# One product of 512 columns in place of two of 256 for the attention's weights times values, with a second addition on VectorE

## The chip, the cores and the metric

The kernel runs on one core of a Trainium2 chip. The metric is the device time of one execution in microseconds (us), the median of several runs. All work is in 4-byte floats. The engines are named as in the profile: PE is TensorE's matmul, PEld its load of the stationary operand, DVE is VectorE, ACT ScalarE, POOL GpSimd, SP SyncE.

## The reference, cut to what matters

One layer of a decoder is computed for a prompt of 1024 tokens and for 8 samples of 8 tokens. The change touches only the attention over the prompt: 8 heads of 64, in blocks of 128 queries, with stick-breaking weights in place of a softmax.

```
z = q @ k.T * HEAD_DIM ** -0.5 + bias
log_beta = log_sigmoid(z)
log_stay = where(causal, log_beta - z, 0)
log_after = reverse_cumsum(log_stay) - log_stay
w = where(causal, exp(log_beta + log_after), 0)
o = w @ v
```

The last line, `w @ v`, is what is done in another way. Before and after it there are dense projections (the input projection ahead of it and beside it, gates, output and feed-forward layers behind it), which the change leaves alone.

## The kernel before, in words

A product of two 4-byte operands is made out of reduced-precision products: each operand is split into a high part (a rounded copy, type fp32r) and a low part (the rest), and high by high, high by low and low by high are added in PSUM. The dense projections (L1126, 364 columns at a time) are such triples.

The heads are taken two at a time: four head pairs, i = 0 to 3, and for each of them 18 dense chunks of the input projection. A unit is one head and one block of 128 queries, so a head pair has 16 units; they come in pairs of the same head and neighbouring query blocks, with 8, 8, 6, 6, 4, 4, 2 and 2 blocks of keys. The order of all engines' work is a list written out ahead (`order`), from which each engine takes its own part, and semaphores hold them together. Slot n of the list has, for different units at once:

- `logits` of unit n+1 on PE (L1276), into banks that the `cap` of the unit before must have read;
- `cap` on DVE (L1893, L1894), `softplus` on ACT (two activations), `suffix` on DVE (the scan L1901 and the subtraction L1903), `weights` on ACT (L1610);
- `turn`: PE transposes the weights in groups of up to four blocks (L1286), ACT copies the result as the high part `th` (L1625), and DVE makes the low part `tl` (`low`, L1911);
- `av`: PE multiplies. The stationary operand `v` is a block of 128 keys by 128 columns, the high part of the 64 values in one half and the low part in the other. The moving operand is `th` and then `tl`, 256 columns (two query blocks), and all blocks of keys are added in 256 columns of bank 7 (`AVB`). For the last block of keys (`top`) only one of the two query blocks exists, so there it is 128 columns;
- `out`: the two halves of the partitions must be added. ACT copies the low half to `otmp` (L1634), and DVE adds it to the high half and writes the result into `br` (L1930). There is one `out` for each pair of units, 8 in a head pair, 32 in all.

Between these, PE has dense products as a filler in every slot. An engine works strictly down its list: what stands behind a waiting instruction waits too. `av` waits for `tl_made` (DVE) and, in a unit pair's first group, for `o_made` of the unit pair before; `logits` waits for `zc_ready` (DVE); `turn` waits for `w_made` (ACT).

Of the kernel before, what the change touches and what calls it, by code (L numbers as in the profile page):

```python
# [33 lines left out]
F32R = mybir.dt.float32r  # L34
I32 = mybir.dt.int32
ALU = mybir.AluOpType
ACT = mybir.ActivationFunctionType

P = 128
# [4 lines left out]
GRAN = 4  # L44
# [6 lines left out]
def ds(start, size):  # L51
    return bass.ds(start, size)


def hybrid_layer(nc, x_prompt, x_sample, cache_k, cache_v, state_conv, page_table, norm1_w, w_in, conv_w,
# [42 lines left out]
    with ctx:  # L98
# [3 lines left out]
        def place(name, shape, dt, at=None):  # L102

            size = 4
            for n in shape[1:]:
                size *= n
            off = cursor[0] if at is None else at
            if at is None:
                cursor[0] += (size + 31) // 32 * 32
            return nc.alloc_sbuf_tensor_at(name, shape, dt, offset=off)  # L110
# [85 lines left out]
        vcu = place("vcu", [P, NV], F32)  # L196
        vhl = place("vhl", [P, NB * 2 * P], F32R)
        sp = [place(f"sp{s}", [P, SEQ], F32) for s in range(2)]
        th = [place(f"th{s}", [P, GRAN * 2 * P], F32R) for s in range(NT)]
        tl = [place(f"tl{s}", [P, GRAN * 2 * P], F32R) for s in range(NT)]  # L200
        stage = [place(f"stage{s}", [P, GRAN * P], F32) for s in range(2)]
        otmp = place("otmp", [P, 2 * P], F32)
        ends = place("ends", [P, NPAIR * N_END], F32)
# [26 lines left out]
        def blocks(t, n=P):  # L230
            return t.rearrange("p (k n) -> p k n", n=n)
# [13 lines left out]
        def bank(b, a=0, e=512):  # L245
            return ps[:, b * 512 + a:b * 512 + e]
# [8 lines left out]
        def sem(name, credit=0):  # L255

            s = ctx.enter_context(nc.semaphore(name))
            if credit:
                credits.append((s, credit))
            return s  # L260
# [24 lines left out]
        stage_made = sem("stage_made")  # L285
        stage_out = [sem(f"stage_out{s}", 1) for s in range(2)]
        vh_made, v_made = sem("vh_made"), sem("v_made")
        otmp_made, o_made = sem("otmp_made"), sem("o_made")
        qs_made, ks_made, k_copied = sem("qs_made"), sem("ks_made"), sem("k_copied")
        cols_in, cols_turned, cols_made = sem("cols_in"), sem("cols_turned"), sem("cols_made")  # L290
        pad_made, conv_step = sem("pad_made"), sem("conv_step")
# [825 lines left out]
        def _(pe):  # L1117
# [77 lines left out]
            for e in order:  # L1195
# [92 lines left out]
                elif e[0] == "av":  # L1288
# [9 lines left out]
                    for b in range(a, z):  # L1298
                        v = vhl[:, (b * 2 + h) * P:(b * 2 + h + 1) * P]
                        x = P if b == top else 0  # L1300
                        at = (b - a) * 2 * P
                        mm(bank(AVB, x, 2 * P), v, th[s][:, at + x:at + 2 * P], start=(b == 0), stop=False)  # L1302
                        ins = mm(bank(AVB, x, 2 * P), v, tl[s][:, at + x:at + 2 * P], start=False, stop=(b == top))  # L1303
                    ins.then_inc(turned_used, 1)


# [456 lines left out]
        def _(v):  # L1763
# [98 lines left out]
            for e in order:  # L1862
# [33 lines left out]
                elif e[0] == "suffix":  # L1896
                    u = e[2]
                    W = width(u)
                    rev = sp[u % 2][:, 0:W][:, ::-1]
                    v.wait_ge(sp_made, i * UNITS + u + 1)  # L1900
                    V_.tensor_tensor_scan(rev, rev, rev, 0.0, ALU.add, ALU.bypass).then_inc(suffix_made, 1)  # L1901
                    v.wait_ge(suffix_made, i * UNITS + u + 1)
                    V_.tensor_tensor(zc[u % NZ][:, 0:W], zc[u % NZ][:, 0:W], sp[u % 2][:, 0:W], ALU.subtract).then_inc(arg_made, 1)  # L1903
                elif e[0] == "low":
                    u, j = e[2:]
                    turn = ("turn", i, u, j)
                    a, z = groups(u)[j]
                    s = both_turned((i, u), j) % NT
                    x = UNIT[u][1] % 2 * P
                    v.wait_ge(th_made, w_no[turn] + 1)  # L1910
                    V_.tensor_tensor(blocks(tl[s], 2 * P)[:, 0:z - a, x:x + P], blocks(bank(TURN + turn_no[turn] % 2, 0, (z - a) * P)),  # L1911
                                     f32(blocks(th[s], 2 * P)[:, 0:z - a, x:x + P]), ALU.subtract).then_inc(tl_made, 1)
                elif e[0] == "v_split":
                    m = 3 + e[2]
                    s = m % 2
                    v.wait_ge(stage_made, i * 6 + m + 1)
                    if e[2] < 2:
                        src = stage[s][:, :].rearrange("p (b h d) -> p b h d", h=2, d=HD)
                        dst = vhl[:, e[2] * GRAN * 2 * P:(e[2] + 1) * GRAN * 2 * P].rearrange("p (b x d) -> p b x d", x=4, d=HD)
                        V_.tensor_copy(dst[:, :, 0:4:3, :], src).then_inc(vh_made, 1)  # L1920
                        v.wait_ge(vh_made, i * 2 + e[2] + 1)
                        V_.tensor_tensor(dst[:, :, 1:3, :], src, f32(dst[:, :, 0:4:3, :]), ALU.subtract).then_inc(v_made, 1)
                    else:
                        V_.tensor_copy(vs[:, ds(i * P, P)], stage[s][0:SMP, 0:P]).then_inc(v_made, 1)
                elif e[0] == "out":
                    u = e[2]
                    h, t = UNIT[u]
                    r = slice(h * HD, h * HD + HD)
                    v.wait_ge(otmp_made, i * NB + u // 2 + 1)
                    V_.tensor_tensor(br[r, ds(i * NTOK + (4 * NTOK + t // 2 * (2 * P)), 2 * P)], ps[r, AVB * 512:AVB * 512 + 2 * P],  # L1930
                                     otmp[r, :], ALU.add).then_inc(o_made, 1)
                elif e[0] == "p1_end":
                    p1_over(v)
                    v.wait_ge(bias_in, 16 * (P // NEW))
                    v.wait_ge(const_step, N_STEPS)
                    V_.memset(qblk[:, :], 0.0).then_inc(qblk_zero, 1)
                    v.wait_ge(qblk_zero, 1)
                    v.wait_ge(qs_made, NPAIR)
                    own_q(0)
                elif e[0] == "page":  # L1940
                    _, j, t = e
                    if by_dve(t):
                        kct_free(v, j, t)
                        v.wait_ge(s_turned, s_no[e] + 1)
                        V_.tensor_copy(blocks(kct[t // GRAN % 2][:, :], 512)[:, :, t % GRAN * P:(t % GRAN + 1) * P],
                                       blocks(bank(TURN + s_no[e] % 2))).then_inc(kct_dve, 1)
                elif e[0] == "s_cap":
                    j = e[1]
                    new = "s_new", j
                    v.wait_ge(s_turned, s_no[new] + 1)  # L1950
                    V_.scalar_tensor_tensor(out=zs_c[:, PAST:KEYS], in0=bank(TURN + s_no[new] % 2, 0, SMP), scalar=bias_s[:, 0:1],
                                            in1=new_cap[:, ds(j * SMP, SMP)], op0=ALU.add, op1=ALU.min).then_inc(new_z_read, 1)
                    V_.tensor_scalar(zs_c[:, 0:PAST], ps[:, ZB * 512:ZB * 512 + PAST], bias_s[:, 0:1], Z_MAX,
                                     ALU.add, ALU.min).then_inc(s_zc, 1)
                    if j + 1 < NITER:
                        own_q(j + 1)
                elif e[0] == "b_split":
                    x = b_part(e[1])
                    v.wait_ge(b_hi, e[1] + 1)
                    V_.tensor_tensor(bl[:, x], br[:, b_source(e[1])], f32(bh[:, x]), ALU.subtract).then_inc(b_lo, 1)  # L1960
                elif e[0] == "b_split_sample":
                    v.wait_ge(b_hi, KT + 1)
                    V_.tensor_tensor(b_sample(bl), b_sample(br), f32(b_sample(bh)), ALU.subtract).then_inc(b_lo, 1)
                elif e[0] == "s_suffix":
                    j = e[1]
                    rev = sp_s[:, :][:, ::-1]
                    v.wait_ge(s_sp, j + 1)
                    V_.tensor_tensor_scan(rev, rev, rev, 0.0, ALU.add, ALU.bypass).then_inc(s_suffix, 1)
                    v.wait_ge(s_suffix, j + 1)
                    V_.tensor_tensor(zs_c[:, :], zs_c[:, :], sp_s[:, :], ALU.subtract).then_inc(s_arg, 1)  # L1970
                elif e[0] == "s_out":
                    _, j, n = e
                    v.wait_ge(s_turned, s_no[e] + 1)
                    for h in range(2):
                        r = slice(h * HD, h * HD + HD)
                        own = n * 2 * NEW + h * NEW
                        src = bank(TURN + s_no[e] % 2, 0, P)[r, :].rearrange("p (w x) -> p w x", x=TILE)[:, :, own:own + NEW]
                        dst = blocks(br[r, :], NTOK)[:, NPAIR:2 * NPAIR, ds(j * (2 * NEW) + (SEQ + n * NEW), NEW)]
                        ins = V_.tensor_copy(dst, src)
                    ins.then_inc(so_made, 1)  # L1980
# [157 lines left out]
```

## Time and profile before

| | |
|---|---|
| median of 3 runs | 1657.03 us (1656.65 to 1657.3) |
| profiled execution, its own time | 1656.68 us |
| its span | 1654.7 us |
| PE busy | 1644.6 us (99%) |
| DVE busy | 694.0 us (42%) |
| ACT busy | 516.9 us (31%) |
| granted TensorE clock | 0.999 of full speed |
| `av` products | 79.6 to 444.3 us of the span |

The duration of one matmul in the profile is its way through the array and is longer than its share of time: matmuls overlap, and what one costs is read from start to start. Idle time of an engine stands in square brackets behind the instruction that ended it, with the one that it waited for.

### The profile page before, as it was taken

The numbers are of one execution on the slowest core, as the hardware profiler recorded it, in microseconds if no ns is written. First come the engines' busy times: TensorE is split into PE (matmuls) and PEld (weight loads), VectorE is DVE, ScalarE is ACT, GpSimd is POOL, SyncE is SP. The second block draws the span as 40 slices with busy tenths as digits, with TensorE's granted clock in tenths as the row PEclk, the third lists the DMA queues.
The fourth block names the chain that finished last, engine by engine and source line by source line (L and its number), as shares of the span: only waits on it lengthen the run. The fifth ranks groups of instructions, "written<-read, shape, count | busy, mean of one in ns | idle before, by whom it ended". The sixth has DMA issues, their size and how long they took to land.

```text
span 1654.7 us, 24985 instructions
## 1 busy us (share of the span) xinstructions
PE 1644.6 (99%) x9956; PEld 1520.6 (92%) x9956; DVE 694.0 (42%) x1156; ACT 516.9 (31%) x1001; POOL 569.2 (34%) x402
## 2 busy tenths in 40 slices
PE   9999999999999999999999999999999999999998
PEld 8999999999988889999889998899888998899987
DVE  7785868859421222466334330032211331022333
ACT  7565655656322222422245220022100220012111
POOL 5212212112212111232884334733347324652510
PEclk9999999999999999999999999999999999999999
DMA  5202112021276677442552111321113111221211
GB/s 161 66 26 68 39 39 73 21 63 42 96 241 196 208 230 228 164 143 91 172 178 77 52 52 64 102 65 50 53 64 115 49 42 64 89 83 46 89 51 57
DMA packets 145006, 157.55 MB, mean 95 GB/s; under 512 B 9119, under 2 KB 99899, under 8 KB 144892
## 3 DMA queue, kind: packets, MB, share of 16 engines
q1 hardware_dynamic: 144746, 155.93, 29.7%
q8 instruction: 79, 1.29, 0.3%
q14 instruction: 35, 0.29, 0.1%
q10 hardware_dynamic: 146, 0.04, 0.0%
HBM read 136.96 MB, written 18.98 MB: 94 GB/s over the span
## 4 chain that ended last, share of the span: by engine, by line
PE 89%; DVE 6%; ACT 3%; issue 1%; POOL 0%; DVEq 0%; ACTq 0%; POOLq 0%
PE ps L1126 51%; PE ps L1418 10%; PE ps L1423 10%; PE ps L1421 9%; DVE sp L1901 2%; PE ps L1320 2%; DVE zc L1893 1%; PE ps L1276 1%; PE ps L1286 1%; PE ps L1364 1%; PE ps L1332 1%; ACT sp L1604 1%; PE ps L1303 1%; PE ps L1302 1%; DVE br L1849 1%
## 5 line engine op out<-in xcount | busy, mean ns | idle before, releaser
L1126 PE MATMUL ps<-xh,wh 128*128 128x364 f32 (+1 forms) x956 | 323.7, 339 | 0.7 <-DVE xl L1874 0.6
L1126 PE MATMUL ps<-xh,wl 128*128 128x364 f32 (+1 forms) x956 | 313.8, 328 | 0.0
L1126 PE MATMUL ps<-xl,wh 128*128 128x364 f32 (+1 forms) x956 | 313.8, 328 | 0.0
L1113 POOL TENSOR_TENSOR wl<-raw,wh 128x1024 fp32r<-128x1024 f32 x106 | 256.3, 2418 | 19.1 <-POOL wh L1110 18.9
L1126 PE MATMUL ps<-yh,wh 128*128 128x384 f32 (+1 forms) x768 | 250.5, 326 | 0.2 <-DVE yl L2070 0.2
L1126 PE MATMUL ps<-yh,wl 128*128 128x384 f32 (+1 forms) x768 | 250.5, 326 | 0.0
L1110 POOL CAST wh<-raw 128x1024 fp32r<-128x1024 f32 x106 | 111.1, 1048 | 404.8 <-issue 383.1
L1126 PE MATMUL ps<-yl,wh 128*128 128x384 f32 (+1 forms) x768 | 250.3, 326 | 0.0
L1728 ACT ACTIVATE ts<-tt 128x384 f32<-128x384 f32 (+1 forms) x96 | 48.8, 508 | 553.8 <-DVE tt L2082 553.7
L1027 POOL CAST wh<-raw 128x1024 fp32r<-128x1024 f32 x48 | 50.8, 1059 | 479.1 <-issue 205.3
L1126 PEld LDWEIGHTS ps<-xh,wh 128*128 128x128 f32 x956 | 179.7, 188 | 17.0 <-issue 15.3
L2018 DVE TENSOR_TENSOR x<-ps,x 128x512 f32<-128x512 f32 x90 | 60.0, 690 | 320.5 <-PE ps L1423 302.2
L1126 PEld LDWEIGHTS ps<-xl,wh 128*128 128x128 f32 x956 | 180.1, 188 | 0.7
L1126 PEld LDWEIGHTS ps<-xh,wl 128*128 128x128 f32 x956 | 179.7, 188 | 0.0
L1418 PE MATMUL ps<-wh,hh 128*128 128x512 f32 x468 | 179.0, 390 | 0.6 <-POOL wl L1113 0.6
L1423 PE MATMUL ps<-wl,hh 128*128 128x512 f32 x468 | 163.4, 389 | 0.0
L1421 PE MATMUL ps<-wh,hl 128*128 128x512 f32 x416 | 161.9, 389 | 0.0
L1036 POOL TENSOR_TENSOR wl<-raw,wh 128x1024 fp32r<-128x1024 f32 x48 | 116.6, 2428 | 97.2 <-DVE zc L1903 91.4
L2082 DVE TENSOR_SCALAR tt<-ps 128x384 f32<-128x384 f32 (+1 forms) x96 | 51.4, 535 | 233.0 <-PE ps L1126 231.6
L1126 PEld LDWEIGHTS ps<-yh,wh 128*128 128x128 f32 x768 | 144.1, 188 | 1.0 <-issue 0.4
L1126 PEld LDWEIGHTS ps<-yl,wh 128*128 128x128 f32 x768 | 144.1, 188 | 0.0
L1126 PEld LDWEIGHTS ps<-yh,wl 128*128 128x128 f32 x768 | 144.1, 188 | 0.0
(190 smaller groups left out, 2632.2 us busy)
## 6 DMA issues: line engine op xcount, KB each, us to landing
raw<-in_w_down SPq DMA_DIRECT2D x112, 256.0 KB, 2.9
raw<-in_w_in SPq DMA_DIRECT2D x80, 256.0 KB, 3.5
cache<-in_cache_k SPq DMA_DIRECT2D x64, 256.0 KB, 3.6
cache<-in_cache_v SPq DMA_DIRECT2D x64, 256.0 KB, 3.7
raw<-in_w_up SPq DMA_DIRECT2D x64, 256.0 KB, 3.2
raw<-in_w_out SPq DMA_DIRECT2D x48, 256.0 KB, 2.9
gates<-gst SPq DMA_DIRECT2D x16, 544.0 KB, 6.0
gb<-gates SPq DMA_DIRECT2D x16, 544.0 KB, 5.7
```

The lines of the kernel that those rows point to most:

```text
L1027: g.tensor_copy(wh[s][:, :], raw[s][:, :]).then_inc(w_hi, 1)
L1036: g.tensor_tensor(wl[s][:, :], raw[s][:, :], f32(wh[s][:, :]), ALU.subtract).then_inc(w_split, 1)
L1110: g.tensor_copy(high[:, :], raw[n % 3][:, :]).then_inc(w_hi, 1)
L1113: g.tensor_tensor(low[:, :], raw[n % 3][:, :], f32(high[:, :]), ALU.subtract).then_inc(w_split, 1)
L1126: ins = mm(out, lhs[:, k * P:(k + 1) * P], rhs[:, x], start=(first and a == 0 and m == 0), stop=(last and a == n - 1 and m == 2))
L1320: ins = tr(bank(tb, p * P, (p + 1) * P), cache[g][:, (a * NPAIR + p) * P:(a * NPAIR + p + 1) * P], ident[:, :])
L1418: mm(out, hi, w, start=k == 0, stop=False)
L1421: mm(out, low[:, k * SEQ + b * P:k * SEQ + b * P + P], w, start=False, stop=False)
L1423: return mm(out, hi, lo_w, start=False, stop=last)
L1728: A(ts_[m % 2][:, 0:z - a], tt[:, 0:z - a], ACT.Square).then_inc(s_made, 1)
L2018: V_.tensor_tensor(x, step_bank(step_no[g, b, h]), x, ALU.add).then_inc(step_free, 1)
L2082: V_.tensor_scalar(tt[:, 0:z - a], step_bank(t, 0, z - a), 0.0, None, ALU.max).then_inc(step_free, 1)
```

## The change

The high and the low part of the turned weights now lie in one tile, `thl`, the low part behind the high one. Each block of keys is one matmul with the high and the low columns side by side as its moving operand: 512 columns, and 256 (written 2x128) for the last block. Bank 7 then holds the products with the high part in its first 256 columns and those with the low part in its last 256. The stationary operand is loaded once instead of twice. `out` has one more addition on DVE: first the high half of the last 256 columns is added to `otmp` (in place), and, after a wait on a new semaphore for that, `otmp` to the high half of the first 256 columns as before. The product of the values' low part with the weights' low part is computed too, as before, but is no longer added to the result.

```diff
-        th = [place(f"th{s}", [P, GRAN * 2 * P], F32R) for s in range(NT)]
-        tl = [place(f"tl{s}", [P, GRAN * 2 * P], F32R) for s in range(NT)]
+
+        thl = [place(f"thl{s}", [P, 2 * GRAN * 2 * P], F32R) for s in range(NT)]
+        th = [w[:, 0:GRAN * 2 * P] for w in thl]
+        tl = [w[:, GRAN * 2 * P:2 * GRAN * 2 * P] for w in thl]
...
-                        mm(bank(AVB, x, 2 * P), v, th[s][:, at + x:at + 2 * P], start=(b == 0), stop=False)
-                        ins = mm(bank(AVB, x, 2 * P), v, tl[s][:, at + x:at + 2 * P], start=False, stop=(b == top))
+                        ins = mm(blocks(bank(AVB, 0, 4 * P), 2 * P)[:, :, x:2 * P], v,
+                                 blocks(thl[s], GRAN * 2 * P)[:, :, at + x:at + 2 * P], start=(b == 0), stop=(b == top))
...
                     v.wait_ge(otmp_made, i * NB + u // 2 + 1)
+                    V_.tensor_tensor(otmp[r, :], ps[r, AVB * 512 + 2 * P:AVB * 512 + 4 * P], otmp[r, :], ALU.add).then_inc(otmp_both, 1)
+                    v.wait_ge(otmp_both, i * NB + u // 2 + 1)
                     V_.tensor_tensor(br[r, ds(i * NTOK + (4 * NTOK + t // 2 * (2 * P)), 2 * P)], ps[r, AVB * 512:AVB * 512 + 2 * P],
                                      otmp[r, :], ALU.add).then_inc(o_made, 1)
```

PE at the first `av` of the program (head pair 0, units 0 and 1, the first group of four blocks and the start of the second), before:

```order
L1126 MATMUL ps<-xl,wh_61 128x364
L1126 MATMUL ps<-xh,wl_63 128x364
L1302 MATMUL ps<-th_124,vhl 128x256
L1303 MATMUL ps<-tl_126,vhl 128x256
L1302 MATMUL ps<-th_124,vhl 128x256
L1303 MATMUL ps<-tl_126,vhl 128x256
```

And in the changed kernel, where two lines more stand ahead of the same code:

```order
L1128 MATMUL ps<-xl,wh_61 128x364
L1128 MATMUL ps<-xh,wl_63 128x364
L1304 MATMUL ps<-thl_124,vhl 128x512 x4
L1304 MATMUL ps<-thl_125,vhl 128x512 x3
L1304 MATMUL ps<-thl_125,vhl 128x2x128
L1288 MATMUL ps<-ident,zc_132 128x128 x8
```

The 16 matmuls of this `av` have become 8, in the same place between the same neighbours.

DVE at the third `out` of head pair 0, between two small copies of the convolution and a low part, before:

```order
L1849 SCALAR_TENSOR_TENSOR br<-vcu,cols,br 128x1024
L1849 SCALAR_TENSOR_TENSOR br<-vcu,cols,br 128x64
L1930 TENSOR_TENSOR br<-ps,otmp 64x256
L1911 TENSOR_TENSOR tl_126<-ps,th_124 128x4x128
L1911 TENSOR_TENSOR tl_127<-ps,th_125 128x128
L1901 SCALAR_TENSOR_TENSOR sp_123<-sp_123 128x384
```

And in the changed kernel:

```order
L1851 SCALAR_TENSOR_TENSOR br<-vcu,cols,br 128x1024
L1851 SCALAR_TENSOR_TENSOR br<-vcu,cols,br 128x64
L1932 TENSOR_TENSOR otmp<-ps,otmp 64x256
L1934 TENSOR_TENSOR br<-ps,otmp 64x256
L1913 TENSOR_TENSOR thl_124<-ps,thl_124 128x4x128
L1913 TENSOR_TENSOR thl_125<-ps,thl_125 128x128
L1903 SCALAR_TENSOR_TENSOR sp_123<-sp_123 128x384
```

Nothing has changed places; one addition stands ahead of the old one, and everything behind it on DVE has one instruction more before it.

## Rows read from the trace of the kernel before

**Rows 1.** The page: span, and busy time of each engine.
```profile
span 1654.7 us, 24985 instructions
...
PE 1644.6 (99%) x9956; PEld 1520.6 (92%) x9956; DVE 694.0 (42%) x1156; ACT 516.9 (31%) x1001; POOL 569.2 (34%) x402
```

**Rows 2.** One line's instructions, L1303: count, shortest, median, longest ns, first and last start, forms.
```profile
L1303 PE MATMUL ps<-tl,vhl x160: 274/283/289, 79.7 to 444.3; 128*128 128x256 f32 x128, 128*128 128x128 f32 x32
```

**Rows 3.** Timeline of PE, one av of eight blocks: start, duration (us), instruction.
```profile
79.60 0.28 PE L1302 MATMUL ps<-th,vhl 128*128 128x256 f32 x1
79.72 0.28 PE L1303 MATMUL ps<-tl,vhl 128*128 128x256 f32 x1
...
81.27 0.22 PE L1302 MATMUL ps<-th,vhl 128*128 128x128 f32 x1
...
81.45 1.06 PE L1286 MATMUL ps<-ident,zc 128*128 128x128 f32 x8
```

**Rows 4.** PE's busy time, instructions and clock in a stretch of 512-column matmuls only.
```profile
1590.00:1640.00 50.00, 50.00 (x222) 1.00 0.19 69
```

**Rows 5.** Busy time by stretch: length, PE, PEld, DVE, ACT, POOL, clock, DMA share, GB/s.
```profile
98.40:126.00 27.60, 27.45 (x187) 26.52 (x186) 26.11 (x51) 16.56 (x36) 3.87 (x4) 1.00 0.07 20
126.00:150.00 24.00, 24.00 (x153) 23.87 (x152) 10.87 (x25) 12.86 (x34) 9.23 (x5) 1.00 0.15 45
```

**Rows 6.** Timeline of DVE in head pair 0, second to sixth out; last, head pair 3.
```profile
98.40 0.43 DVE L1930 TENSOR_TENSOR br<-ps,otmp 64x256 f32<-64x256 f32 x1 [1.00 <-ACT otmp L1634]
...
101.63 0.88 DVE L1911 TENSOR_TENSOR tl<-ps,th 128x512 fp32r<-128x512 f32 x2
...
110.59 0.41 DVE L1930 TENSOR_TENSOR br<-ps,otmp 64x256 f32<-64x256 f32 x1
110.92 0.87 DVE L1911 TENSOR_TENSOR tl<-ps,th 128x512 fp32r<-128x512 f32 x2
...
113.56 0.34 DVE L1894 SCALAR_TENSOR_TENSOR zc<-ps,bias_p,diag_cap 128x128 f32<-128x128 f32 x1
...
115.92 0.43 DVE L1930 TENSOR_TENSOR br<-ps,otmp 64x256 f32<-64x256 f32 x1 [0.21 <-ACT otmp L1634]
...
118.36 0.56 DVE L1911 TENSOR_TENSOR tl<-ps,th 128x384 fp32r<-128x384 f32 x1
...
123.89 0.40 DVE L1930 TENSOR_TENSOR br<-ps,otmp 64x256 f32<-64x256 f32 x1
124.34 0.56 DVE L1911 TENSOR_TENSOR tl<-ps,th 128x384 fp32r<-128x384 f32 x1
...
131.54 0.43 DVE L1930 TENSOR_TENSOR br<-ps,otmp 64x256 f32<-64x256 f32 x1 [0.89 <-ACT otmp L1634]
132.00 0.29 DVE L1911 TENSOR_TENSOR tl<-ps,th 128x128 fp32r<-128x128 f32 x1
...
433.47 0.29 DVE L1911 TENSOR_TENSOR tl<-ps,th 128x128 fp32r<-128x128 f32 x1
```

**Rows 7.** Timeline of PE and its loads at the matmuls behind those; last, head pair 3.
```profile
102.16 0.33 PE L1126 MATMUL ps<-xh,wl 128*128 128x364 f32 x1
...
102.46 0.35 PE L1302 MATMUL ps<-th,vhl 128*128 128x256 f32 x1
...
113.96 0.38 PE L1276 MATMUL ps<-kx,qd 128*128 128x256 f32 x1
...
119.06 0.35 PE L1302 MATMUL ps<-th,vhl 128*128 128x256 f32 x1
...
125.09 0.19 PEld L1302 LDWEIGHTS ps<-th,vhl 128*128 128x128 f32 x1
...
132.41 0.19 PEld L1302 LDWEIGHTS ps<-th,vhl 128*128 128x128 f32 x1
...
435.25 0.29 PE L1302 MATMUL ps<-th,vhl 128*128 128x256 f32 x1
```

More of the change, by code:

```diff
@@ L287, in hybrid_layer @@
         vh_made, v_made = sem("vh_made"), sem("v_made")
-        otmp_made, o_made = sem("otmp_made"), sem("o_made")
+        otmp_made, otmp_both, o_made = sem("otmp_made"), sem("otmp_both"), sem("o_made")
         qs_made, ks_made, k_copied = sem("qs_made"), sem("ks_made"), sem("k_copied")
```

## The prediction

> **What bounds the kernel now.** I read the page first. PE is busy for 1644.6 us of a span of 1654.7 [rows 1], so the kernel is bound by PE nearly everywhere, and a change is worth what it takes from or adds to PE's stream: matmul time, or time in which PE waits. The matmuls that change, 160 blocks of keys, lie in the first quarter of the span, from 79.6 to 444.3 us [rows 2], and there I looked for the engine that PE would wait for. The busy time by stretches names it. From the second `out` of head pair 0 to 126 us DVE is busy for 26.11 us of 27.60, against 10.87 of 24.00 in the stretch behind [rows 5]. In the first of these two DVE has no slack to speak of, while PE still looks full (27.45). The timelines of both engines then show how close they run: the next sections go through them.
>
> **What it takes from PE.** An `av` of eight blocks has 14 matmuls of 256 columns in 81.27 - 79.60 = 1.67 us, 0.119 us each, and its two matmuls of 128 columns take 81.45 - 81.27 = 0.18 us [rows 3]. Matmuls of 512 columns, where there is nothing else, come every 50.00 / 221 = 0.226 us [rows 4]. So a full block goes from 2 x 0.119 to 0.226 us and saves 0.012 us; the number of columns is the same, and only the fixed part of one matmul goes away. The second load of the stationary operand costs nothing before either: it runs beside the matmul. The last block goes from 0.18 us to one matmul of 256 columns, 0.12 us, and saves 0.06 us. With 128 full and 32 last blocks [rows 2] that is 1.5 + 1.9 = 3.4 us for PE in all, 0.14, 0.12, 0.10 and 0.07 us for an `av` of eight, six, four and two blocks.
>
> No row shows a moving operand of two pieces 1024 elements apart. I take it at the price of a contiguous one, 0.226, since the columns are the same in number and bank 7 is written in one piece. The bound on the other side is two matmuls of 256 columns, 0.238: then the full blocks save nothing and 1.9 us are left.
>
> The trace is to be weighed against a rule here. The Trainium skill, page "TensorE: Matmul & The Clock Gate", section "Back-to-back issue gap", gives a sustained 81 ns per matmul of 128 columns and 131 ns for 512, so that wide matmuls would be far cheaper per column; by an estimate between its two figures a block would go from about 195 to 131 ns, and PE would save some 8 us on the full blocks. The rows give 226 ns, so the trace does not agree, and the sum goes by the rows.
>
> **What it adds to DVE.** 32 additions of 64x256 from PSUM, the same shape as the one that is there, which takes 0.40 to 0.43 us [rows 6]. The new one is followed by a wait for its own end, so it counts in full with the semaphore's way: 0.45 us, the step from the `out` at 123.89 to the low part at 124.34, or from 131.54 to 132.00 (0.46) [rows 6]. The lower bound is the step where the next instruction does not have to wait, 110.59 to 110.92, 0.33 us [rows 6]. I take 0.45, since the second addition reads what the first writes. In all 14.4 us on DVE; the question is how much of it reaches PE. The Trainium skill, page "VectorE: DVE Perf Modes", section "The DRAIN you can't avoid", says that a semaphore between two instructions costs nothing beyond the pipeline's own drain; by it the two additions without a wait ahead of the old successor would cost 0.33 each, 0.12 less. The rows show both steps, 0.33 and 0.45, and the forecast uses the longer.
>
> **Which of the eight places reach PE.** The eight `out`s of a head pair, in order:
>
> - The first is absorbed: before the second DVE has stood idle for 1.00 us [rows 6].
> - The second (98.40) has the scan, the subtraction and the low part at 101.63 behind it, and PE already waits for that low part: from 102.16 to 102.46 it takes 0.30 us where the pace of 364 columns is 0.167 [rows 6, 7]. So all of 0.45 reaches PE.
> - The third (110.59) stands before the `cap` that ends at 113.56 + 0.34 = 113.90, and PE starts the logits that need it at 113.96 [rows 6, 7]: 0.45 again.
> - The fourth (115.92) stands before the low part that ends at 118.36 + 0.56 = 118.92; PE's `av` starts at 119.06 [rows 6, 7]: 0.45. The 0.21 us of idle before it is a wait for ACT, which itself runs behind DVE there, and gives nothing back.
> - The fifth (123.89) stands before the low part that ends at 124.90; PE's load for the `av` comes at 125.09, 0.19 us later [rows 6, 7]; the next case shows 0.12 to be enough. Slack 0.07, so 0.38 reaches PE.
> - The sixth (131.54) stands directly before the low part that ends at 132.29, and PE loads at 132.41 [rows 6, 7]: 0.45. In head pair 3 PE comes to this `av` only at 435.25, with the low part made at 433.47 + 0.29 = 433.76, so there it is absorbed [rows 6, 7].
> - The seventh and eighth are absorbed: DVE is less than half busy there [rows 5].
>
> Between the second and the fifth DVE never catches up, as its busy share shows, and what PE saves in the `av`s there only makes it wait longer. So per head pair PE loses 3 x 0.45 + 0.38 + 0.45 = 2.18 us (1.73 in head pair 3). It keeps its saving where it is the bound: two `av`s of eight, one of four, two of two blocks, 2 x 0.14 + 0.10 + 2 x 0.07 = 0.52 us. Net 3 x 1.66 + 1.21 = 6.2 us more.
>
> The other stages are not touched, and all of them come behind PE, so the delay stays. The profiled execution took 1656.68 us and the median is 1657.03, 0.35 above; on the median the sum is 1657.0 + 6.2 = 1663.2, and I say 1663.
>
> What is queued behind the new wait on DVE is what was named for each place; PE's `av` also waits for `o_made`, which comes 0.45 us later, but it is made before the low part for which the same `av` waits, so it is not what is late. ACT's next copy to `otmp` waits for `o_made` too, a slot later.
>
> **The rivals.**
>
> - *DVE's additions stay hidden.* For it: DVE is busy for only 42% of the span [rows 1], and at two of the places DVE stands idle for 1.00 and 0.89 us right before [rows 6]. Against it: 102.46 and 113.96, where PE waits for DVE already. It decides if PE's stops there are made by something else that has slack. Time: 1657.0 - 3.4 = 1653.6. A wide matmul that is cheaper than 0.226 would take it lower: at 0.20 by 128 x 0.026 = 3.3 us more, 1650.3. Chance 0.08 for both together, since the rows speak against both. The rule of the Trainium skill on the sustained pace, above, is of this second kind.
> - *Half of it is absorbed.* The added instruction costs 0.33 in place of 0.45, and one or two of the places have a slack that I don't see: 4 x (3 x 0.33 - 0.52) = 1.9, 1658.9, within what can't be told from no change. Chance 0.20.
> - *All additions reach PE*: 32 x 0.45 = 14.4 less the saving of 3.4 is +11, 1668. A PE that is held up more often would set this off, since `logits`, `turn` and `av` hand on a delay in a ring (PE, DVE, ACT, PE). Chance 0.07.
> - The forecast, five places (four in the last head pair), 1660.4 to 1666: chance 0.65.
>
> **The numbers.** A measurement of this kernel tells about 0.2%, 3.3 us, from no change. Slower by more than that is the forecast and the rival above it, 0.72; within it 0.20; faster 0.08, since even the full saving of 3.4 us is only just past the bound. The range: down to 1658, which takes in most of the half-absorbed case, up to 1667, the forecast's upper end and part of the last rival. The price of the addition (0.33 to 0.46) alone moves the sum by 19 x 0.12 = 2.3 us.
>
> **What the profile after would show.** `av` of eight blocks in about 1.72 us where it was 1.85; 512 columns from start to start in 0.226 to 0.23 us. The new addition 0.40 to 0.43 us, the old one 0.45 behind it. PE's stop before the `av` behind the second `out` 0.6 us long where it was 0.13, and one of about 0.5 us more before the logits behind the third; each head pair some 1.6 us longer. No second stop at the seventh and eighth. I would be wrong if PE's stops do not grow by the addition's length at 102.46 and 113.96 (then something else holds it), or if the wide matmul's pace is not that of 512 contiguous columns.

## The result, and the profile after

The changed kernel takes 1672.37 us (median of 4, 1670.36 to 1672.76), the kernel before 1657.16: a ratio of 1.0089, 95% interval 1.0072 to 1.0107. It is slower by 15.2 us. The forecast was 1663 with a range of 1658 to 1667: the direction was right, the size was not. The profiled execution took 1670.36 us, the shortest of the four; its span is 13.7 us longer than that of [rows 1].

What the prediction had worked out is there. The page's two lines that answer to [rows 1]:

```profile
span 1668.4 us, 24697 instructions
...
PE 1646.4 (99%) x9796; PEld 1512.5 (91%) x9796; DVE 717.0 (43%) x1188; ACT 516.4 (31%) x1001; POOL 568.6 (34%) x402
```

PE has 160 matmuls fewer. The timeline of PE at the `av` of eight blocks, which answers to [rows 3], and at the first place where it waited for DVE, which answers to the first two rows of [rows 7]:

```profile
79.42 1.87 PE L1304 MATMUL ps<-thl,vhl 128*128 128x512 f32 x8
81.13 1.03 PE L1288 MATMUL ps<-ident,zc 128*128 128x128 f32 x8
...
101.75 0.33 PE L1128 MATMUL ps<-xh,wl 128*128 128x364 f32 x1
102.50 0.70 PE L1304 MATMUL ps<-thl,vhl 128*128 128x512 f32 x2 [0.42 <-DVE thl L1913]
```

The `av` takes 81.13 - 79.42 = 1.71 us (forecast 1.72), which is seven matmuls of 512 columns at 0.227 us and one of 256 at 0.12, and the matmul before the next one stands for 0.75 us where its pace is 0.167, a stop of 0.58 (forecast 0.6, 0.13 before).

What the prediction had not worked out stands 30 us later. The timeline of DVE and POOL from the sixth `out` of head pair 0 on answers to the last rows of [rows 6]:

```profile
132.62 0.43 DVE L1932 TENSOR_TENSOR otmp<-ps,otmp 64x256 f32<-64x256 f32 x1 [0.89 <-ACT otmp L1636]
133.08 0.43 DVE L1934 TENSOR_TENSOR br<-ps,otmp 64x256 f32<-64x256 f32 x1
133.54 0.29 DVE L1913 TENSOR_TENSOR thl<-ps,thl 128x128 fp32r<-128x128 f32 x1
133.65 1.04 POOL L1029 CAST wh<-raw 128x1024 fp32r<-128x1024 f32 x1 [4.19 <-issue]
133.75 1.21 DVE L1903 TENSOR_TENSOR_SCAN sp<-sp 128x128 f32<-128x128 f32 x1
134.86 2.40 POOL L1038 TENSOR_TENSOR wl<-raw,wh 128x1024 fp32r<-128x1024 f32 x1 [0.18 <-POOL wh L1029]
134.99 2.42 DVE L1905 TENSOR_TENSOR zc<-zc,sp 128x128 f32<-128x128 f32 x1
```

The same places in the kernel before:

```profile
132.21 0.41 DVE L1901 TENSOR_TENSOR_SCAN sp<-sp 128x128 f32<-128x128 f32 x1
132.66 0.29 DVE L1903 TENSOR_TENSOR zc<-zc,sp 128x128 f32<-128x128 f32 x1
132.81 1.04 POOL L1027 CAST wh<-raw 128x1024 fp32r<-128x1024 f32 x1 [4.45 <-issue]
134.03 2.40 POOL L1036 TENSOR_TENSOR wl<-raw,wh 128x1024 fp32r<-128x1024 f32 x1 [0.18 <-POOL wh L1027]
```

A scan of 128 columns takes 1.21 us in place of 0.41, and a subtraction of 128 columns 2.42 in place of 0.29. Both end just behind an instruction of POOL: the scan at 134.96, behind the cast's end at 134.69, the subtraction at 137.41, behind 137.26. Before, DVE was through at 132.95, as POOL's cast had just begun. Of the scan's own 0.41 us 0.27 lie behind POOL's end, of the subtraction's own 0.29 us 0.15 do: in both, all but 0.14 us of the instruction's own duration comes only when POOL is done. POOL's own instructions keep their 1.04 and 2.40 us. At half speed each, DVE's subtraction would have been through after some 0.6 us. The Trainium skill, page "SBUF — State Buffer", section "Who interferes with whom", says that a DVE instruction with two inputs in SBUF contends with a GpSimd instruction that reads SBUF, for a read interface that the two share, and its section "SBUF: two separate sides" that it is a lock and not a split of bandwidth; the trace agrees in both, by the figures just given. An instruction that reads one of its inputs from PSUM is not held: in the kernel before, POOL's subtraction runs from 134.03 to 136.43, and DVE's `qz` inside it takes 1.08 us, as it does at 139.65 in the changed kernel, where POOL is idle:

```profile
135.20 1.08 DVE L1798 SCALAR_TENSOR_TENSOR qz<-ps,qd 64x364 fp32r<-64x364 f32 x2 [2.25 <-ACT qd L1535]
```

The kernel before has a hold of this kind too, 11 us earlier. Its scan of 256 columns, which takes 0.68 us elsewhere, takes 0.96 here and ends 0.54 behind a cast of POOL (120.89 + 1.04 = 121.93):

```profile
120.89 1.04 POOL L1027 CAST wh<-raw 128x1024 fp32r<-128x1024 f32 x1 [16.60 <-DVE zc L1903]
...
121.51 0.96 DVE L1901 TENSOR_TENSOR_SCAN sp<-sp 128x256 f32<-128x256 f32 x1
```

The chain of waits of the changed kernel shows what this delay does (start, length, what):

```profile
134.99 2.43 DVE zc L1905
...
137.66 0.07 ACT qd L1537
...
140.20 0.55 DVE qz L1800
140.75 0.14 issue
140.88 1.23 PE ps L1128 x6
```

ACT works strictly down its list: the exponential of unit 15 (L1612) waits for the subtraction, and behind it stand the copies of the next head pair's queries (`qd`, L1537), which begin at 137.66 where they began at 133.20. DVE's `qz` waits for them, and PE for the bank that `qz` frees:

```profile
138.63 0.27 PE L1288 MATMUL ps<-ident,zc 128*128 128x128 f32 x1
140.88 0.40 PE L1128 MATMUL ps<-xh,wh 128*128 128x364 f32 x1 [1.98 <-DVE qz L1800]
```

The waits of PE in the stretch 79:450 are, in the changed kernel (who waited for whom: us in all, times, longest):

```profile
PE ps L1128 <- DVE qz L1800: 5.9, 3, 2.0
PE ps L1304 <- DVE thl L1913: 5.4, 15, 0.5
PE ps L1278 <- DVE zc L1896: 1.1, 4, 0.3
```

The last two lines are the kind of wait that the forecast had, though not quite in its places. At the third `out` it had one stop of about 0.5 us before the logits. The trace has two, 0.22 us before the low part's `av` at 112.22 and 0.26 before the logits at 114.43, and the second is there without any addition as well (0.25 at 114.00 in the first experiment): PE comes earlier by what the product saves. The first line is new and occurs once in each of head pairs 0 to 2, since behind the last one there are no next queries to copy. In head pair 0 the matmul before the stop starts at 138.63 and the one behind it at 140.88, 2.25 us later; less the 0.06 us of a 128-column matmul, a stop is 2.2 us.

There is a third part. The granted clock, 1.00 in the whole of the stretch before, fell for 3.4 us after the second of these stops. Windows of the changed kernel (length, PE busy and instructions, clock, DMA share, GB/s):

```profile
240.00:245.00 5.00, 3.59 (x22) 1.00 0.34 96
245.00:250.00 5.00, 4.43 (x17) 0.66 0.04 12
...
245.90:249.20 3.30, 3.30 (x13) 0.50 0.00 0
```

At 0.50, which is 1.2 GHz of 2.4, PE did 13 matmuls in 3.30 us; without the stop it does 22 in the same window (shown below). The first 13 matmuls behind this stop take 3.78 us (245.57 to 249.35), those behind the third stop, at full clock, 2.23 (351.81 to 354.04): the stretch costs some 1.5 us. The granted clock over the span is 0.998 in this profiled execution (1670.36 us) and 0.997 in the other three (1672.28 to 1672.76), which fits one more such stretch in each of them: 3.3 us at half clock lower the mean by 0.001. They have no trace that shows it, and they are longer by 1.9 to 2.4 us, which is more than one stretch.

### The profile page after: what moved, and what is told of

It reads as the page before. It is cut to its first block, busy times and chain, and to the rows that moved or that the text cites. A ratio compares the mean times of both kernels' runs of the same rounds, so it can differ in the third digit from the quotient of the medians.

```text
span 1668.4 us, 24697 instructions
## 1 busy us (share of the span) xinstructions
PE 1646.4 (99%) x9796; PEld 1512.5 (91%) x9796; DVE 717.0 (43%) x1188; ACT 516.4 (31%) x1001; POOL 568.6 (34%) x402
## 4 chain that ended last, share of the span: by engine, by line
PE 82%; DVE 11%; ACT 4%; issue 2%; POOL 0%; DVEq 0%; ACTq 0%; POOLq 0%
PE ps L1128 46%; PE ps L1420 10%; PE ps L1425 10%; PE ps L1423 9%; DVE sp L1903 3%; PE ps L1322 2%; DVE thl L1913 1%; DVE zc L1895 1%; DVE zc L1905 1%; PE ps L1304 1%; PE ps L1366 1%; PE ps L1334 1%; ACT sp L1606 1%; PE ps L1278 1%; DVE br L1851 1%
```

## The experiments

The first four kernels take the two halves of the change apart, take the collision away, and put one addition at one place. Each time is given with that of the kernel before as it was measured beside it.

**The wide product alone.** The second addition is left out, so the product with the weights' low part is made but not added.

```diff
                     v.wait_ge(otmp_made, i * NB + u // 2 + 1)
-                    V_.tensor_tensor(otmp[r, :], ps[r, AVB * 512 + 2 * P:AVB * 512 + 4 * P], otmp[r, :], ALU.add).then_inc(otmp_both, 1)
-                    v.wait_ge(otmp_both, i * NB + u // 2 + 1)
```

> The changed kernel without the second addition in `out` (the product with the weights' low part is made but not added to the result). Forecast's terms: only PE's saving is left, 3.4 us in all, of which the 0.12 us and 0.10 us of the av products in the stretch where DVE sets the pace only make PE wait longer, so 2 us at least: 1653.6 to 1655. If a moving operand of two pieces 1024 elements apart is dearer than a contiguous one (rival): av of eight blocks takes 1.85 us or more and the time is 1657 or above.

Measured: 1654.79 us (1654.29 to 1655.06) against 1656.57, ratio 0.9988 (0.9979 to 0.9997). The product gives back 1.8 us. That is the forecast's term for the places where PE is the bound, 4 x 0.52 = 2.1; a dearer operand of two pieces is out. From the first `av` to the first dense matmul behind the last one the profile has 362.80 us, against 364.81 before. The `av` of eight blocks takes 81.59 - 79.86 = 1.73 us:

```profile
79.86 1.90 PE L1304 MATMUL ps<-thl,vhl 128*128 128x512 f32 x8
81.59 0.27 PE L1288 MATMUL ps<-ident,zc 128*128 128x128 f32 x1
```

POOL and DVE already touch here, without an addition: the cast begins at 132.49, 0.32 us earlier than before, and the subtraction at 132.53 takes 1.14 us. PE has no stop for `qz` from it.

**The addition alone**, on the kernel before: the old addition is made twice, the second waiting for the first.

```diff
+                    if u in (1, 3, 5, 7, 9, 11, 13, 15):
+                        V_.tensor_tensor(br[r, ds(i * NTOK + (4 * NTOK + t // 2 * (2 * P)), 2 * P)], ps[r, AVB * 512:AVB * 512 + 2 * P],
+                                         otmp[r, :], ALU.add).then_inc(otmp_both, 1)
+                        v.wait_ge(otmp_both, i * 8 + (1, 3, 5, 7, 9, 11, 13, 15).index(u) + 1)
```

> The kernel before with one more 64x256 addition of the same shape on DVE in every `out`, the old one waiting for it; the products stay as before. Theory of the collision (DVE's scan and subtraction behind the sixth `out` now fall on POOL's split of the V weights, stand still until it is over, and ACT and then PE wait): the whole loss is here, 1672 to 1676, with PE standing some 2 us near 138.6, 243 and 350 us. Rival, the product is what costs: 1657 to 1664.

Measured: 1664.95 us (1664.69 to 1668.61), ratio 1.0049 (1.0034 to 1.0065). My expectation of 1672 to 1676 was wrong, and the profile says why: here the starts of DVE's scan and of POOL's cast lie within hundredths of a microsecond, and one execution has it go either way. The profiled execution is the slow one of the four, 1668.61; the timelines of DVE and POOL in its head pairs 0 and 2:

```profile
134.06 1.04 POOL L1027 CAST wh<-raw 128x1024 fp32r<-128x1024 f32 x1 [4.29 <-issue]
134.08 1.30 DVE L1901 TENSOR_TENSOR_SCAN sp<-sp 128x128 f32<-128x128 f32 x1
135.42 2.40 DVE L1903 TENSOR_TENSOR zc<-zc,sp 128x128 f32<-128x128 f32 x1
...
344.64 1.26 POOL L1027 CAST wh<-raw 128x1024 fp32r<-128x1024 f32 x1 [4.30 <-issue]
344.65 0.41 DVE L1901 TENSOR_TENSOR_SCAN sp<-sp 128x128 f32<-128x128 f32 x1
345.10 0.95 DVE L1903 TENSOR_TENSOR zc<-zc,sp 128x128 f32<-128x128 f32 x1
```

In head pair 0, and likewise in head pair 1, POOL got its way, and the whole collision follows; PE has two stops of 2.0 us. In head pair 2 DVE did, as the durations show, although the cast's start is written 0.01 us ahead of the scan's: the scan runs at its usual 0.41, the cast is the longer one (1.26 in place of 1.04), and the subtraction is held only to the cast's end, 0.95. The other three executions (1664.69 to 1664.97) are 8.1 to 8.4 us above the kernel before, which is the forecast's price of the additions without any collision: 6.2 net and 2.1 of saving make 8.3. They have no trace; that they had no stop for `qz` is inferred from this sum and from the 3.7 us between them and the profiled one, nearly two stops.

**The collision taken away.** The changed kernel, with POOL's split of the V weights held back until DVE has done the subtraction of unit 15.

```diff
             def high_before(n):
 
                 i, k = divmod(n, 6)
+                if k == V and i > 0:
+                    return i - 1, 15
                 return (i - 1, 11) if k == K else None
```

> The changed kernel with one more condition on POOL: the high part of the V weights (head pairs 1 to 3) is made only when DVE has finished the subtraction of unit 15 of the head pair before. Theory of the collision: the scan and subtraction behind the sixth `out` take 0.41 and 0.29 us again, PE's three stops of 2.2 us are gone and so are the stretches at half clock that they bring: 1661 to 1664, near the forecast's 1663. Rival, the additions are handed on in a ring of PE, DVE and ACT and POOL has nothing to do with it: the stops stay, 1672.

Measured: 1663.32 us (1663.08 to 1663.51), ratio 1.0040 (1.0024 to 1.0055), 9.05 us below the changed kernel and 6.75 above the kernel before, where the forecast's sum was 6.2. (The changed kernel was 15.2 us above the kernel before as measured beside it; by that the wait takes away 8.5 us.) The timeline of DVE and POOL, and PE's window that had been at half clock:

```profile
134.85 0.41 DVE L1905 TENSOR_TENSOR_SCAN sp<-sp 128x128 f32<-128x128 f32 x1
135.30 0.29 DVE L1907 TENSOR_TENSOR zc<-zc,sp 128x128 f32<-128x128 f32 x1
...
135.85 1.04 POOL L1029 CAST wh<-raw 128x1024 fp32r<-128x1024 f32 x1 [5.31 <-DVE zc L1907]
```

```profile
245.90:249.20 3.30, 3.30 (x22) 1.00 0.00 0
```

and PE's waits, with no line for `qz`:

```profile
PE ps L1306 <- DVE thl L1915: 5.5, 15, 0.5
PE ps L1280 <- DVE zc L1898: 1.1, 4, 0.3
```

The profiles close the sum. From the first `av` to the first dense matmul behind the last one there are 364.81 us before, 370.67 here and 378.75 in the changed kernel. Without the collision that is 5.9 us more, by the forecast 6.2. The collision adds 8.1, and three stops of 2.2 us and one stretch at half clock make 3 x 2.2 + 1.5 = 8.1. From the scan of unit 15 in head pair 0 to that in head pair 1 there are 100.91 us before, 102.49 here (1.6 more, as forecast) and 104.69 in the changed kernel, 2.20 more again.

The ring of PE, DVE and ACT as a cause of its own is out: the additions are all still there, and 9 of the 15 us are gone with one wait on POOL.

**One addition, in the sixth `out` only**, on the kernel before (the same edit as above with `if u in (11,)`).

> The kernel before with the extra addition only in the sixth `out` of each head pair. The scan behind it then starts at about 132.66, 0.15 us ahead of POOL's cast at 132.81, and the subtraction at 133.1, in the cast. Theory of the collision: the subtraction is held to the cast's end at 133.85 but is through before POOL's own subtraction at 134.03, so the stop of PE is short, 0 to 0.4 us: 3 x (0.45 + 0 to 0.4) = 1.4 to 2.6, 1658.4 to 1659.6. Forecast without any collision: 1658.4. If the collision is already whole here: 3 x 2.6 = 8 and some loss of clock, 1665 to 1669.

Measured: 1658.10 us (1657.73 to 1658.60) against 1656.57, ratio 1.0009 (0.9999 to 1.0018): 1.5 us, as the forecast's 3 x 0.45 has it, at the edge of what the measurement tells. The scan is ahead of the cast and takes 0.41, the subtraction behind it 0.94:

```profile
132.89 0.41 DVE L1901 TENSOR_TENSOR_SCAN sp<-sp 128x128 f32<-128x128 f32 x1
133.03 1.11 POOL L1027 CAST wh<-raw 128x1024 fp32r<-128x1024 f32 x1 [4.45 <-issue]
133.34 0.94 DVE L1903 TENSOR_TENSOR zc<-zc,sp 128x128 f32<-128x128 f32 x1
```

**Two additions in the sixth `out`**, the same edit with the addition in a loop of two.

> The kernel before with two extra additions in the sixth `out` of each head pair, one more than in the run before. Theory of the collision: the scan behind them now starts near 133.3, after POOL's cast at about 133.0, so it is held to the cast's end and the subtraction to the end of POOL's own subtraction; PE stops for some 2 us in head pairs 0 to 2, and each such stop can bring 3.4 us at half clock, which cost 1.6: 3 x (0.9 + 2.0) = 8.7 and up to 3 x 1.6, so 1665 to 1670. Without a collision the price stays that of waiting in line: 3 x 0.9 = 2.7, 1659.3.

Measured: 1665.77 us (1665.27 to 1665.91) against 1656.80, ratio 1.0053 (1.0038 to 1.0068): 9.0 us. The second addition costs 7.5 us where the first cost 1.5. The timeline of DVE and POOL:

```profile
133.26 1.04 POOL L1027 CAST wh<-raw 128x1024 fp32r<-128x1024 f32 x1 [4.44 <-issue]
133.59 0.99 DVE L1901 TENSOR_TENSOR_SCAN sp<-sp 128x128 f32<-128x128 f32 x1
134.61 2.40 DVE L1903 TENSOR_TENSOR zc<-zc,sp 128x128 f32<-128x128 f32 x1
```

and of PE's waits the one for `qz`:

```profile
PE ps L1126 <- DVE qz L1798: 5.0, 3, 1.7
```

The step lies where the scan's start passes the cast's. The granted clock did not fall in this profiled execution, although PE stood idle for 1.7 us three times; so the stops bring the fall in some cases only.

**The additions at the second to fifth `out`** (`if u in (3, 5, 7, 9)`).

> The kernel before with the extra addition only in the second to fifth `out` of each head pair, where DVE sets the pace. Forecast's terms: 4 x (3 x 0.45 + 0.38) = 6.9, 1663.5, PE's stops behind the second, third and fourth `out` longer by the addition; DVE meets PE again at 128 us and there is no collision. Rival (the additions cost only in the sum of all): less than 1660.

Measured: 1663.17 us (1662.76 to 1663.50), ratio 1.0038 (1.0025 to 1.0052): 6.4 us of the forecast's 6.9. The four places are measured only together.

**At the first, seventh and eighth** (`if u in (1, 13, 15)`).

> The kernel before with the extra addition only in the first, seventh and eighth `out` of each head pair. Forecast's terms: absorbed, 1656.6 to 1657.2, no stop of PE that was not there before. If DVE's idle time there is not slack: up to 12 x 0.45 = 5.4, 1662.

Measured: 1656.97 us (1656.67 to 1657.64), ratio 1.0001 (0.9992 to 1.0010): absorbed. The three parts, 1.5, 6.4 and 0.2, make 8.1 us, what the additions cost together without a collision.

**The wide product only where its addition is absorbed.** The second addition stands behind the same `if u in WIDE`.

```diff
+        WIDE = (1, 13, 15)
...
+                        if u in WIDE:
+                            ins = mm(blocks(bank(AVB, 0, 4 * P), 2 * P)[:, :, x:2 * P], v,
+                                     blocks(thl[s], GRAN * 2 * P)[:, :, at + x:at + 2 * P], start=(b == 0), stop=(b == top))
+                        else:
+                            mm(bank(AVB, x, 2 * P), v, th[s][:, at + x:at + 2 * P], start=(b == 0), stop=False)
+                            ins = mm(bank(AVB, x, 2 * P), v, tl[s][:, at + x:at + 2 * P], start=False, stop=(b == top))
```

> The wide product and the second addition only for the first, seventh and eighth pair of units of each head pair (av of eight, two and two blocks), where the additions should be absorbed; the other pairs of units as before. Forecast's terms: 4 x (0.14 + 0.07 + 0.07) = 1.1 us less than before, 1655.5, with everything that is absorbed staying so. If the additions are not absorbed there: 1657 or above.

Measured: 1655.86 us (1655.35 to 1657.21) against 1656.80, ratio 0.9995 (0.9986 to 1.0004). It is 0.9 us less by the medians, which the measurement can't tell from nothing.

**Control: POOL's extra wait on the kernel before.**

> Control for the run in which POOL's split of the V weights waits for DVE's subtraction of unit 15: the same condition on the kernel before. Theory of the collision: before, the scan and subtraction are through at 132.95 and the cast starts at 132.81, so there is hardly a collision to remove: 1656.5 to 1657.3. If the condition is worth something by itself (rival: the gain of 9 us in that run came from POOL's later work, not from the collision): 1655 or below.

Measured: 1656.94 us (1656.54 to 1657.63) against 1656.51, ratio 1.0002 (0.9992 to 1.0012). The wait itself is worth nothing; in the third experiment it was worth 9 us because there was a collision to take away.

**The distance between the two engines in all of them.** Head pair 0: the start of POOL's cast less the start of DVE's scan of unit 15, and the durations of the scan and the subtraction, in us:

| kernel | distance | scan | subtraction | stop of PE for `qz` |
|---|---|---|---|---|
| before | 0.60 | 0.41 | 0.29 | none |
| additions at the second to fifth | 0.46 | 0.41 | 0.29 | none |
| wide product alone | 0.41 | 0.41 | 1.14 | none |
| one addition in the sixth | 0.14 | 0.41 | 0.94 | none |
| additions alone, head pair 2 | -0.01 | 0.41 | 0.95 | none |
| additions alone | -0.02 | 1.30 | 2.40 | 2.0 |
| changed kernel | -0.10 | 1.21 | 2.42 | 2.0 |
| two additions in the sixth | -0.33 | 0.99 | 2.40 | 1.7 |

The stop comes with the scan that is held, and a held subtraction of 1.14 us costs PE nothing. Both halves of the change use the distance up: the addition at the sixth place takes 0.46, those before it 0.14, and the product 0.19, each measured alone; together that would leave -0.19, and the changed kernel has -0.10. In the kernel's code the cast waits for a dense product of PE (`dense_done` in `split`), and PE is there sooner when the product has saved it time. The additions alone only come up to zero; with the product the changed kernel is past it in all three head pairs.

## Why the prediction was right in part, and where it failed

- **The product's saving**, 4 x 0.52 = 2.1 us: 1.8 measured by itself. Right, and the rows' pace of 0.226 us for 512 columns was the one to go by. The rule of the Trainium skill on the sustained pace (page "TensorE: Matmul & The Clock Gate", section "Back-to-back issue gap") would have made more of it, and no run here shows that.
- **The price of an addition**, 0.45 us: right. The changed trace has 98.43 - 97.97 = 0.46 from the new addition to the old at the second `out`:

```profile
97.97 0.43 DVE L1932 TENSOR_TENSOR otmp<-ps,otmp 64x256 f32<-64x256 f32 x1 [1.00 <-ACT otmp L1636]
98.43 0.43 DVE L1934 TENSOR_TENSOR br<-ps,otmp 64x256 f32<-64x256 f32 x1
```

- **Which places reach PE**: right for each group, not shown for each place. Second to fifth 6.9 forecast, 6.4 measured; the sixth by one addition 1.4 and 1.5; the first, seventh and eighth 0 and 0.2. Without the collision the sum of 6.2 us meets the 6.75 of the third experiment, 5.9 within its profile's `av` stretch.
- **The step that failed** is the sixth place: "The sixth (131.54) stands directly before the low part that ends at 132.29 [...]: 0.45." I followed the added time from there only to the low part that PE waits for. Behind the low part stand the scan and the subtraction of unit 15, and I took their durations as fixed. The trace before had both signs: POOL's cast begins 0.14 us before that subtraction's end, and ACT has the next queries' copies behind the exponential of the same unit. The hold itself could be read there too, in the scan at 121.51. With the additions DVE is later against PE by more than POOL is, POOL comes first, and the two DVE instructions last 3.63 us in place of 0.70, which makes 2.2 us of stop in each of three head pairs on top of the 0.45. "The seventh and eighth are absorbed: DVE is less than half busy there" came out right for the additions there, but idle time of DVE did not take in what the sixth had set off: DVE's 2.25 us of idle before `qz` are time behind ACT, and they are there in both kernels. POOL does not appear in the prediction's argument at all. The kernel before had a third sign: POOL's splits of other weights wait for a subtraction of DVE (`behind`, and `high_before` for the keys' weights, in its code), and the page shows POOL standing idle 91.4 us for them; the split of the V weights has no such wait.

```profile
L1036 POOL TENSOR_TENSOR wl<-raw,wh 128x1024 fp32r<-128x1024 f32 x48 | 116.6, 2428 | 97.2 <-DVE zc L1903 91.4
```

- **What it cost**: the third experiment puts it at 9.05 us (1672.37 less 1663.32), or 8.5 with each against the kernel before beside it. Three stops of 2.2 us are 6.6, shown in the trace. The rest, 1.9 to 2.4, fits one to two stretches at half clock of some 1.5 us each. One is in the profiled trace, where the sum closes at 8.1; for the other executions it is inferred from their mean clock alone.
- **The rivals**: the upper one, 1668 by all additions reaching PE, came nearest in height, 4 us short, with the wrong mechanism; the first, seventh and eighth additions never reach it.

## What to carry to other kernels

When an instruction is added to an engine, follow the shift to the next point where that engine meets each other engine, and there look not only at who waits by a semaphore but also at pairs of instructions that hold each other up without one. Here these were VectorE's scan and subtraction, both with all inputs in SBUF, against GpSimd's cast and subtraction, which read SBUF. Where such a pair is some tenths of a microsecond apart (0.60 here), a shift of that size (0.70) costs the length of GpSimd's instructions and not of the shift, and then whatever stands in line behind the held result. Whatever makes the other engine earlier uses up the same distance. An explicit wait that orders the two cost nothing that could be measured here (the ninth experiment), and gave 9 us back where they met. A wait between two engines that the kernel has at some places and not at others is a hint of such a pair.

The other half: joining two matmuls of 256 columns with the same stationary operand saves only the fixed part of one, 0.012 us of 0.238 here (0.06 for two of 128); it is no payment for an addition of 0.45 us on an engine that sets the pace, unless that addition falls where the engine is idle.

## What the hardware showed unexpectedly

- DVE and POOL hold each other up in both directions: where the scan kept its 0.41 us, the cast that started with it took 1.26 us in place of 1.04; where the cast kept its 1.04, the scan took 1.30. A held instruction of DVE ends behind POOL's by its own duration less 0.14 us, in the scan of 128 columns (0.27), that of 256 (0.54) and the subtraction (0.15). At starts 0.01 to 0.02 us apart the profile's order of the starts does not tell who is held.
- The same kernel has executions at 1664.7 and at 1668.6 us, with a mean clock of 0.999 and 1.00. The trace shows the two outcomes of that race in one execution; that the race makes the 4 us between executions is inferred.
- Stops of PE of 1.7 to 2.0 us: in the second experiment's profile and with two additions in the sixth `out` the granted clock stayed at 1.00; in the changed kernel it fell to 0.50 for 3.4 us after one of three. The mean clock is 0.997 or 0.998 in all four executions of the changed kernel and 0.999 or 1.00 in all four of each of the other two. What decides it is open.
